# Weight and operand loads from one queue, zero-filling on VectorE, and the order of VectorE's work in a float32 hybrid encoder's MLP

## The reference

```python
def squared_relu_mlp(h, w_up, w_down):          # w_up 1024 x 4096, w_down 4096 x 1024
    return jnp.square(jax.nn.relu(h @ w_up)) @ w_down

h = h + rmsnorm(mix, norm_mix_post[l])
ff = squared_relu_mlp(rmsnorm(h, norm_mlp_pre[l]), w_up, w_down)
h = h + rmsnorm(ff, norm_mlp_post[l])
```

## Time and profile before

| | us |
|---|---|
| median of 3 runs | 2308.46 (2307.14 to 2309.11) |
| the profiled execution | 2309.11 |
| its span | 2307.4 |
| PE busy | 2231.9 (97%) |
| DVE busy | 1651.9 (72%) |
| ACT busy | 697.7 (30%) |
| POOL busy | 624.5 (27%) |

### The profile page before, as it was taken

How to read it: one execution, slowest core, us unless ns; L and a number is a source line. 1 busy time by engine, 2 the same in 40 slices (tenths; PEclk the granted TensorE clock), 3 DMA queues, 4 the chain that set the end, 5 groups by cost and what they waited for, 6 DMA issues and landing times.

```text
span 2307.4 us, 34577 instructions
## 1 busy us (share of the span) xinstructions
PE 2231.9 (97%) x13856; PEld 2019.0 (88%) x13856; DVE 1651.9 (72%) x1638; ACT 697.7 (30%) x828; POOL 624.5 (27%) x387
## 2 busy tenths in 40 slices
PE   7999999998999999999999999999989999999997
PEld 6999989998999999999989999877777777787787
DVE  6788644665868877977587887354768779778868
ACT  4564433340211211221254653242512112211212
POOL 3333215023222222122414432151232222222240
PEclk9999999999999999999999999999999999999998
DMA  4111002355543554542241111022556544653514
GB/s 136 33 58 39 29 26 89 92 192 209 206 175 136 204 183 155 183 171 77 83 140 46 51 37 37 20 94 80 201 185 225 187 180 152 227 182 122 196 56 146
DMA packets 122673, 290.73 MB, mean 126 GB/s; under 512 B 9552, under 2 KB 29264, under 8 KB 122576
## 3 DMA queue, kind: packets, MB, share of 16 engines
q1 hardware_dynamic: 50032, 153.30, 19.4%
q10 hardware_dynamic: 72544, 136.06, 16.9%
HBM read 251.25 MB, written 38.08 MB: 125 GB/s over the span
## 4 chain that ended last, share of the span: by engine, by line
PE 72%; DVE 14%; issue 5%; DMA 5%; ACT 2%; POOL 1%; DVEq 0%; SPq 0%; POOLq 0%; ACTq 0%
PE banks L802 30%; PE banks L1072 17%; PE banks L1042 9%; PE banks L933 5%; PE banks L854 2%; DMA w_raw<-w_units 2%; DMA r<-w_units 2%; DVE w_hl L2260 2%; POOL w_hl L679 1%; PE banks L857 1%; DVE hid L2278 1%; DVE sum_lo L2291 1%; PE banks L842 1%; PE banks L841 1%; PE banks L1172 1%
## 5 line engine op out<-in xcount | busy, mean ns | idle before, releaser
L802 PE MATMUL banks<-X,w_hl 128*128 128x348 f32 (+2 forms) x3744 | 648.8, 332 | 2.3 <-ACT ki L1558 1.8
L802 PEld LDWEIGHTS banks<-X,w_hl 128*128 128x128 f32 x3744 | 605.7, 188 | 30.2 <-issue 7.5
L1072 PE MATMUL banks<-sum_hi,w_hl 128*128 128x260 f32 (+1 forms) x1440 | 317.4, 325 | 24.4 <-DVE sum_lo L2291 20.0
L1042 PE MATMUL banks<-X,w_hl 128*128 128x260 f32 (+1 forms) x1944 | 316.6, 322 | 7.4 <-DVE w_hl L2260 7.4
L1042 PEld LDWEIGHTS banks<-X,w_hl 128*128 128x128 f32 x1944 | 281.4, 190 | 37.8 <-issue 8.0
L654 POOL TENSOR_SCALAR w_hl<-w_raw 128x1024 fp32r<-128x1024 f32 x70 | 91.7, 1310 | 789.9 <-issue 528.3
L1072 PEld LDWEIGHTS banks<-sum_hi,w_hl 128*128 128x128 f32 x1440 | 227.1, 191 | 53.3 <-issue 26.9
L679 POOL TENSOR_SCALAR w_hl<-r 128x1024 fp32r<-128x1024 f32 x72 | 112.6, 1564 | 361.8 <-DVE r L2249 128.6
L656 POOL TENSOR_TENSOR w_hl<-w_raw,w_hl 128x1024 fp32r<-128x1024 f32 x70 | 201.9, 2885 | 5.8
L1072 PE MATMUL banks<-sum_lo,w_hl 128*128 128x260 f32 (+1 forms) x720 | 192.7, 322 | 0.0
L1630 ACT ACTIVATE hid<-banks 128x1040 f32<-128x1040 f32 (+1 forms) x48 | 49.7, 1035 | 368.8 <-PE banks L1042 368.8
(11 more groups left out here) (239 smaller groups left out, 3766.5 us busy)
## 6 DMA issues: line engine op xcount, KB each, us to landing
w_raw<-w_units SPq DMA_DIRECT2D x148, 512.0 KB, 3.5
r<-w_units SPq DMA_DIRECT2D x84, 512.0 KB, 3.8
X<-t_mem ACTq DMA_DIRECT2D x56, 520.0 KB, 6.7
X<-t_mem ACTq DMA_DIRECT2D x56, 512.0 KB, 6.7
X<-t_mem SPq DMA_DIRECT2D x16, 520.0 KB, 5.7
t_extra<-t_mem ACTq DMA_DIRECT2D x16, 520.0 KB, 7.7
X<-t_mem SPq DMA_DIRECT2D x16, 512.0 KB, 5.1
t_extra<-t_mem ACTq DMA_DIRECT2D x16, 512.0 KB, 7.1
```

Of the source, the lines that this page charges most:

```text
L802: ins = nc.tensor.matmul(out[:, b, 0:t.width(b)], wp, xp[:, t.used(b)], start=first and n == 0, stop=last and n == 2)
L1042: ins = nc.tensor.matmul(banks[:, first + b, 0:t.block], wp, xp[:, b * t.block:(b + 1) * t.block], start=opens and (half, kk, i) == (0, 0, ...
L1072: ins = nc.tensor.matmul(out[:, m + b, :], wp, xp[:, k, b * t.block:(b + 1) * t.block], start=k == 0 and i == 0, stop=k == 1 and i == 2)
```

## The change

It has five parts.

1. In the middle groups all loads of T (and in the last group of b12) are issued by SP, in the order written below; ACT issues none there. ACT's loop now holds all six groups.
2. The six Z accumulators are zeroed by DVE, behind the eight down copies of group 0, and not by POOL.
3. `x_sums(1)` moves ahead of the first down copy, and the four `x_low(1, ...)` stand one each behind down copies 2 to 5.
4. At the entry the low part of UP_A11 moves from ahead of the last down copy to behind the memsets and Y's two subtractions; the first weight sum stands behind it.
5. In the middle groups the low part of UP_A22 moves behind the weight sums DN_S3 and DN_S2, and the low part of X_T3 moves ahead of the relu of UP_4's result.

```diff
 # SP
             def middle_group(l, g, last):
...
                 sp.wait_ge(t_half_used, 4 * n + 1)
-                t_load_high(l, 0, T2, 1)
+                t_load(l, 0, T2, 1)
...
                 when_split(UP_S4)
                 raw_load(l, g, 2, 0, Q_A22)
+                sp.wait_ge(up_done, products + UP_5 + 1)
+                t_load(l, 1, T3, 0)
+                sp.wait_ge(t_half_used, 4 * n + 2)
+                t_load(l, 2, T3, 1)
                 when_split(UP_S3)
                 raw_load(l, g, 1, 1, Q_A22)
-                sp.wait_ge(t_half_used, 4 * n + 2)
-                t_load_high(l, 2, T3, 1)
+                sp.wait_ge(up_done, products + UP_6 + 1)
+                t_load(l, 0, T4, 0)
...
                 sp.wait_ge(t_half_used, 4 * n + 3)
-                t_load_high(l, 1, T4, 1)
+                t_load(l, 1, T4, 1)
+                if not last:
+                    sp.wait_ge(up_done, products + UP_7 + 1)
+                    t_load(l, 2, T2, 0)
...
 # POOL
                 pool.wait_ge(t_stored, 16 * 20 * (l + 1))
-                for z in (*Z1, *Z5, *Z6):
-                    nc.gpsimd.memset(z[:, :, :], 0.0).then_inc(z_zeroed, 1)
...
 # DVE, group 0 and the entry
                 group(0, l * NJ + J_MLP, l * COUNTED_TILES)
+                x_sums(1)
                 dve.wait_ge(h_stored, 16 * (2 * NX * l + kept.pieces))
                 for m in range(KT):
-                    if m == KT - 1:
-                        weights_low(1, UP_A11)
                     down_sum(m, l * NJ + J_MLP, True)
-                    if m == 0:
-                        x_sums(1)
-                    if 1 <= m < 3:
-                        x_low(1, 2 * m - 2)
-                        x_low(1, 2 * m - 1)
+                    if 2 <= m < 6:
+                        x_low(1, m - 2)
+                dve.wait_ge(t_stored, 16 * 20 * (l + 1))
+                for z in (*Z1, *Z5, *Z6):
+                    V.memset(z[:, :, :], 0.0).then_inc(z_zeroed, 1)
...
-                first_up_sum(1)
                 dve.wait_ge(z_zeroed, 6 * (l + 1))
                 dve.wait_ge(y_spread, 2 * (l + 1))
+                weights_low(1, UP_A11)
+                first_up_sum(1)
...
 # DVE, a middle group
                     relu(0, (0, 1))
-                    weights_low(g, UP_A22)
...
                     weights_sum(g, SUM_DN_S2, 3, 1, 3, ALU.subtract)
+                    weights_low(g, UP_A22)
...
                     weights_low(g, DN_S3)
+                    low(X_T3, t3[:, :, 0:t.width])
                     dve.wait_ge(up_done, PRODUCTS * n + UP_4 + 1)
...
-                    low(X_T3, t3[:, :, 0:t.width])
```

More of the change, by code:

```diff
@@ L540, in t_load @@
                     sp.dma_start(t_slot(l, place, s).bitcast(f32), t_part(l, t, half, s)).then_inc(t_loaded[place], 16)
-            def t_load_high(l, place, t, half):
-                sp.dma_start(t_slot(l, place, 0).bitcast(f32), t_part(l, t, half, 0)).then_inc(t_loaded[place], 16)
             def middle_group(l, g, last):
-                n = groups_before(l, g)
+                n, products = groups_before(l, g), PRODUCTS * groups_before(l, g)
                 def when_split(operand):
@@ L572, in middle_group @@
                 raw_load(l, g, 0, 1, Q_A12)
+                for place, used in ((0, (t_half_used, 4 * n + 4)), (1, (up_done, products + PRODUCTS))):
+                    sp.wait_ge(*used)
+                    if not last:
+                        t_load(l, place, T1, place)
+                        continue
+                    for s in range(2):
+                        sp.dma_start(t_slot(l, place, s).bitcast(f32), b12_part(l, place, s)).then_inc(b12_loaded, 16)
                 when_split(DN_A11)
@@ L1611, in hidden, with middle_group @@
                     nc.scalar.activation(act_hi[:, i, c], T[2 + i % 2][:, c], ACT.Copy).then_inc(a_hi, 1)
-                def middle_group(g, last):
+                def middle_group(g):
                     n = groups_before(l, g)
[L1617 to L1625, removed]
                     def copied(product, chain, q):
@@ L1647, in middle_group @@
                     copied(UP_1, 0, (0, 0))
-                    when_half_used(1)
-                    t_load(0, T2, 1, (1,))
                     copied(UP_5, 1, (1, 0))
-                    t_load(1, T3, 0)
-                    when_half_used(2)
-                    t_load(2, T3, 1, (1,))
                     copied(UP_6, 0, (0, 1))
-                    t_load(0, T4, 0)
                     square(0, (0, 1))
-                    when_half_used(3)
-                    t_load(1, T4, 1, (1,))
                     copied(UP_7, 0, (1, 1))
-                    if not last:
-                        t_load(2, T2, 0)
                     square(1, (1, 1))
@@ L1666, in middle_group @@
                     square(3, (1, 0))
[L1667 to L1674, removed]
                     high(X_B11, quarter(l, (0, 0)))
@@ L1720, in _ @@
                 store_lows(1)
-                with act.Fori(1, MIDDLE) as g:
-                    middle_group(g, False)
-                middle_group(MIDDLE, True)
+                with act.Fori(1, GROUPS - 1) as g:
+                    middle_group(g)
                 act.wait_ge(h_stored, 16 * (2 * NX * l + out.pieces))
```

## The result

The changed kernel takes 2392.58 us (median of 4 runs, 2387.88 to 2397.24), the kernel before 2307.8 (2306.15 to 2309.11): ratio 1.0368, 95% interval 1.0346 to 1.0390, so 85 us or 3.7% slower. The forecast was 2380, in a range of 2338 to 2414.

A forecast was written before the change was run, and what follows sets the result against it. PE, busy 97% of the span, was taken as the bound, so added PE waits count. Terms 16.4 + 7 + 41 + 1.5 + 7 - 1 = 72 on 2309.1 us gave 2380, range 2338 to 2414.

The forecast's parts named there:

- Entry: Entry of the middle groups: UP_A11 behind memsets and subtractions, PE idles 11.7 us; +8.2 per layer, +16.4 us.
- Group 0: Group 0, both layers: sums from `x_scaled` delay the first down copy and PE; +7 us, ends 3 and 10.
- Part 3: Twelve middle groups: later loads put PE's down products 3.0 or 3.9 us later per group, +41 us before smaller terms.
- step (a): Middle groups: raw 1, issued behind both halves of T3, lands 0.6 to 1.5 us later, taken as +1.0.
- step (b): Middle groups: UP_A22's low part behind S3 and S2 delays r2's load; S4 starts 3.0 us later, 3.9 in layer 1.
- (d): Middle groups: longer PE idle brings the low clock, mostly absorbed in layer 0; +7 us, ends 0 and 15.
- A stall of 1 to 1.6 us: Middle groups: PE waits for T4's second half, but ahead of the longer `sum_lo` wait, so no added cost.
- (c): Layer 0 middle groups: X_T3's `sum_lo` ahead of the relu, one 1.2 us operation later, mostly absorbed; +1.5 us.
- Rival 1: Steady groups hide the later load, only the entry and group 0 cost: 2332 us, chance 0.12.
- Rival 2: Middle groups: one queue is slower than two, raw 1 lands 4 us later, 48 us more: 2428, chance 0.10.
- Rival 3: Middle groups: one queue in order lands raw 1 over 4.4 us earlier, gaining time: 2300 us, chance 0.03.

The follow-up runs named there:

- b_order: Kernel before with only the entry's changed DVE order, the six memsets left on POOL: 2310.89 us, ratio 1.0015.
- b_x0: Kernel before with only group 0's reordered sums and low parts from `x_scaled`: 2315.11 us, ratio 1.0032.
- b_queue: Kernel before with only the queue edit in the middle groups, SP issuing all T loads: 2327.66 us, ratio 1.0086.
- b_a22: Kernel before with only UP_A22's low part moved behind the sums S3 and S2: 2348.63 us, ratio 1.0172.
- g_t4: Kernel before with all edits inside the middle groups, but SP loads T4's second half ahead of the wait for UP_A22's split: 2375.9 us, ratio 1.0298.
- b_groups: Kernel before with all edits inside the twelve middle groups and no others: 2374.54 us, ratio 1.0287.
- b_x3: Kernel before with only X_T3's low part ahead of the relu of b21: 2310.45 us, ratio 1.0003.
- q_raw1: Kernel before with all T loads on SP, and raw 1 issued ahead of both halves of T3: 2302.33 us, ratio 0.9976.
- b_hold: Kernel before, both queues kept, with ACT holding the load of T3's first half until UP_S3 is split: 2297.57 us, ratio 0.9957.
- a_raw1: Whole changed kernel, but SP issues raw 1 ahead of both halves of T3: 2374.25 us, ratio 1.0281 to the kernel before.

## Why the prediction was right, and where it was off

- **Entry, +16.4.** Right: +14.3 alone. The memset's price, taken as 1.1, is 0.93 busy at a spacing of 1.09; PE's wait is 11.5 for 11.7 worked out. That the memsets stand in front of UP_A11 is the cause (`b_order`). The clock's share was right too: it moves from UP_5 to UP_1 and keeps its size. The product behind the wait, first in the changed kernel, then in the kernel before (columns as in the earlier trace rows):

```profile
569.40:576.80 7.40, 7.40 (x49) 7.40 (x50) 7.23 (x6) 0.00 (x0) 3.72 (x2) 0.77 0.00 0
```
```profile
564.00:571.40 7.40, 7.35 (x48) 7.36 (x49) 4.14 (x3) 0.00 (x0) 2.47 (x2) 0.77 0.15 36
```

The longer stretch at the lower level is the wait itself: from 562.6 to 569.3 PE does nothing and the granted clock is 0.50, which costs nothing.
- **Group 0, +7.** +7.3 alone, though only +2.7 in the trace of the changed kernel. The mechanism held, with both of its ends: the first copy is late behind DVE's sums, by more where one of them meets POOL's operation (`b_x0`). Where between its ends a run falls was not forecast, so the closeness of +7.3 to +7 is in part luck.
- **Part 3, +48.5 with its clock and small terms.** Direction and mechanism held, the size was low: +66 alone. The table shows the chain in four runs, in us from the group's start; each cell has layer 0 and layer 1, the mean of the five groups past the first.

| | S1 starts | S3 starts | S4 starts | first down product | whole group |
|---|---|---|---|---|---|
| kernel before | 21.8, 20.9 | 27.9, 27.4 | 33.1, 31.8 | 42.1, 40.7 | 85.2, 80.7 |
| `b_queue` | 23.9, 23.8 | 30.3, 30.1 | 34.0, 33.7 | 42.9, 42.6 | 86.1, 82.6 |
| `b_a22` | 21.8, 20.8 | 27.9, 27.1 | 35.3, 35.3 | 44.2, 44.2 | 87.2, 85.2 |
| changed kernel | 23.9, 23.9 | 30.3, 30.1 | 37.7, 37.5 | 47.2, 46.6 | 90.2, 86.3 |

The mis-sized term is step (a), raw 1. It was taken as +1.0 with ends at +0.6 and +1.5; S1 starts 2.1 us later in layer 0 and 3.0 in layer 1, and in the group shown its load takes 8.2 us, not 7.6. S3 follows it, +2.4 and +2.7 where the forecast had +0.6. From S3 to S4 the forecast had 7.3 us, and they are 7.4: step (b) was right in itself. So S4 is 4.6 and 5.7 us later, not 3.0 and 3.9, which is 20 us over the twelve groups, against a miss of 66 - 48.5 = 18. The edits apart point less clearly: (a) costs 19 where the low end of the forecast had 12, and (b) 40 where its increments to S4 (2.0 in layer 0, 2.9 in layer 1) make 29.
- **(d), the clock, +7.** The earlier trace rows shows the lower level behind a wait of 3.7 us only. In the trace of the kernel before it begins within 1.5 us of the end of eight of the nine PE waits between 2.0 and 3.7 us, so the reading was sound. The changed kernel's clock falls elsewhere than forecast, on the second half of UP_4 in both layers: some 2 us a group, most of PE's 25 us of longer busy time. But PE would have waited for `sum_lo` there. The first down product starts 0.5 us (layer 0) and 0.2 (layer 1) later than `sum_lo`'s own delay accounts for: 4 us in all, an estimate from the same timelines. `g_t4` agrees: there that product runs at full speed (48 matmuls in 5.90 us), and the first down product starts only 0.2 us earlier than in `b_groups`.
- **"A stall of 1 to 1.6 us, but it ... costs nothing more."** This sentence failed as a size. T4's second half is issued 1.5 us later than worked out. Its first load lands 5.4 us after that, as forecast, but the second, for which PE waits too, only 8.0 after it. The stall is 4 to 5 us. That it lies ahead of the wait for `sum_lo` was right, and `g_t4` shows that without it the sum stays as it is. But the sign that the forecast named, a `sum_lo` wait of 4.5 us before every first down product, did not show: these waits fell to 4.5 us in all, because the wait for the T load stands in front of them. The time came out as forecast, this part of the picture did not.
- **(c), +1.5:** +2.0 by the medians and +0.7 by the ratio, which allows -1.8 to +3.2. That later waits of the chain absorb most is what the rows of `b_x3` show.
- **Rivals.** Rival 1 (groups hide it) is out by `b_groups`. Rival 2 (a slower queue) put raw 1 some 5 us later than before and named over 3 us more of idle time before S1 as its sign. In the group shown it is 1.9 more, in the mean of the groups 2.2 in layer 0 and 3.0 in layer 1, so layer 1 is at the edge of that sign; but `q_raw1` shows that one queue in another order is no slower than the two of the kernel before. Rival 3, one queue bringing raw 1 early, was refused rightly for this order of loads; but its mechanism is real. `q_raw1` does just this and gains.

The parts alone sum to 14.3 + 7.3 + 66.2 = 88, against 85 measured together. Inside the groups 19.3 + 40.3 + 2.0 = 62, against 66. This near agreement hides two larger differences, which the table shows. In layer 0 the two edits cost 0.9 and 2.0 us a group apart, but 5.0 together in the changed kernel: S4 had 1.5 us of idle time before it, which takes up most of the queue edit's delay of S3 as long as UP_A22 is split early, and none once it is split behind S3. In layer 1 they cost 1.9 and 4.5 apart and 5.65 together; there `b_a22` also loses 1.0 us behind the first down product, after waits of 3.6 to 4.7 us for `sum_lo` with the clock at its lower level behind them, which the changed kernel does not lose at that place.

## What to carry to other kernels

When a step is moved behind another that waits for a load, ask which load its own end releases: a transfer that ran beside the sums ahead of it is then issued behind them, and what they waited for is paid first. A wait named in the profile may only be the first of two that end together; take it away alone before you call it the cause. And with a queue in order, put the load that somebody waits for now ahead of the ones wanted later; in `b_hold` what the other queue was given at that moment delayed it as well.

## What the hardware showed beyond that

- A DVE memset of 128x1040 float32 is busy 0.93 us, but the next starts only 1.09 after it: six take 6.4 us from the first start to the last end. POOL's six take 5.51.
- A load of 512 KB takes 3.5 us to land when alone. The load of raw 1 takes 7.5 us in the kernel before, 3.8 when 1.06 MB in the other queue are held back, and 8.2 behind 2.1 MB of T3 in its own queue with earlier loads still under way. S3's load takes 7.1 us in `a_raw1`, issued behind 3.2 MB of T3 and T4.
- Behind a wait of 4 to 5 us in the middle of dense matmuls, half a product took 4.4 to 5.6 us in place of 3.0, in all twelve groups. Whether that costs time depends on what PE would wait for next: here most of it was covered by the wait for `sum_lo`.
